# Modulation tiles out of the weight ring: three slots for weights on SP's queue, one slot for modulation tiles on GpSimd's queue

## What is computed

```python
mod = (s_lat @ ada_w[l] + ada_b[l])[:, None, :]      # s_lat = silu(c)
sh1, sc1, g1, sh2, sc2, g2 = jnp.split(mod, 6, axis=-1)
h = modulate(rmsnorm(x, norm1_g[l]), sh1, sc1)       # h * (1 + scale) + shift
...                                                  # h @ w_in: attention, Fourier mix, long convolution
x = x + g1 * (y @ w_out[l])
x = x + g2 * conv_gated_mlp(modulate(rmsnorm(x, norm2_g[l]), sh2, sc2), *ffn)
```

## Time and profile before

| what | value |
|---|---|
| median of 3 runs | 2317.23 us |
| the profiled execution: its own time | 2316.17 us |
| the profiled execution: span of its instructions | 2314.4 us |
| mean granted TensorE clock | 0.986 |
| DMA, all on queue q1 | 467.12 MB, 60.9% of 16 engines' span |

### The profile page before, as it was taken

One profiled execution on the slowest core, in us unless ns is written; L12 is line 12 of the kernel. 1 busy time (PEld: TensorE's weight loads), 2 busy tenths in 40 slices (PEclk: granted clock), 3 DMA queues, 4 the chain that ended last, 5 costly groups with the idle time before them and its releaser, 6 DMA issues.

```text
span 2314.4 us, 37963 instructions
## 1 busy us (share of the span) xinstructions
PE 2202.2 (95%) x16510; PEld 2040.4 (88%) x16510; DVE 1467.1 (63%) x1802; ACT 1029.1 (44%) x1393; POOL 6.2 (0%) x10
## 2 busy tenths in 40 slices
PE   7999999899999997988999799979999999999997
PEld 7889998789899997988788689979999999998885
DVE  6666647757656786767665377776666665555654
ACT  6554334334454553444333354544444443444453
POOL 0000000000000000000000000000000000000000
PEclk9999999999999999999999899989999999999998
DMA  8766565565447876867564655647676766555552
GB/s 295 242 208 193 176 205 182 166 211 164 128 130 253 273 247 200 279 218 252 175 202 154 173 184 184 235 134 264 221 238 219 238 224 205 188 183 198 184 200 91
DMA packets 344260, 469.55 MB, mean 203 GB/s; under 512 B 20445, under 2 KB 318301, under 8 KB 331102
## 3 DMA queue, kind: packets, MB, share of 16 engines
q1 hardware_dynamic: 344094, 467.12, 60.9%
HBM read 465.00 MB, written 2.10 MB: 202 GB/s over the span
## 4 chain that ended last, share of the span: by engine, by line
PE 61%; DVE 6%; ACT 3%; DMA 2%; issue 1%; SPq 1%; DVEq 0%; ACTq 0%
PE ps L1781 14%; PE ps L1779 14%; PE ps L1780 14%; PE ps L1791 3%; PE ps L1793 3%; PE ps L1792 3%; DVE wlo L1087 2%; ACT whi L558 2%; DVE arena L1150 1%; DMA raw<-w_in_dram 1%; SPq L491 1%; PE ps L1802 1%; PE ps L1803 1%; PE ps L1801 1%; PE ps L2142 1%
## 5 line engine op out<-in xcount | busy, mean ns | idle before, releaser
L1087 DVE TENSOR_TENSOR wlo<-raw,whi 128x1024 fp32r<-128x1024 f32 (+1 forms) x668 | 814.3, 1221 | 791.7 <-ACT whi L558 789.7
L558 ACT ACTIVATE whi<-raw 128x1024 fp32r<-128x1024 f32 (+1 forms) x668 | 703.3, 1055 | 1054.5 <-PE ps L1781 836.8
L1779 PE MATMUL ps<-phi,whi 128*128 128x256 f32 (+2 forms) x3744 | 1084.7, 290 | 23.8 <-DVE wlo L1087 15.6
L1780 PE MATMUL ps<-plo,whi 128*128 128x256 f32 (+2 forms) x3744 | 1057.5, 282 | 0.0
L1781 PE MATMUL ps<-phi,wlo 128*128 128x256 f32 (+2 forms) x3744 | 1057.1, 282 | 0.0
L1779 PEld LDWEIGHTS ps<-phi,whi 128*128 128x128 f32 (+1 forms) x3744 | 709.3, 189 | 62.8 <-issue 33.4
L1780 PEld LDWEIGHTS ps<-plo,whi 128*128 128x128 f32 (+1 forms) x3744 | 706.5, 189 | 8.2 <-issue 7.1
L1781 PEld LDWEIGHTS ps<-phi,wlo 128*128 128x128 f32 (+1 forms) x3744 | 709.8, 190 | 0.3
L1150 DVE SCALAR_TENSOR_TENSOR arena<-raw,cst,arena 128x1024 f32<-128x1024 f32 x120 | 153.5, 1280 | 3.4 <-DMA raw<-ada_w_dram 0.3
L1791 PE MATMUL ps<-whi,dhi 128*128 128x512 f32 x352 | 136.9, 389 | 0.0
L1793 PE MATMUL ps<-wlo,dhi 128*128 128x512 f32 x352 | 136.9, 389 | 0.0
(11 more groups left out here) (340 smaller groups left out, 2347.9 us busy)
## 6 DMA issues: line engine op xcount, KB each, us to landing
raw<-w_in_dram SPq DMA_DIRECT2D x151, 1024.0 KB, 6.1
raw<-ada_w_dram SPq DMA_DIRECT2D x96, 1024.0 KB, 5.0
raw<-ffn_w_up_dram SPq DMA_DIRECT2D x88, 1024.0 KB, 5.1
raw<-ffn_w_down_dram SPq DMA_DIRECT2D x44, 1024.0 KB, 5.2
raw<-w_out_dram SPq DMA_DIRECT2D x32, 1024.0 KB, 6.1
raw<-w_branch_dram SPq DMA_DIRECT2D x16, 1024.0 KB, 5.6
arena<-xT_dram SPq DMA_DIRECT2D x4, 544.0 KB, 6.5
arena<-ctxT_dram SPq DMA_DIRECT2D x1, 2048.0 KB, 10.0
```

The lines of the kernel that those rows point to most:

```text
L558: nc.scalar.activation(whi[c % 4][:, 0:w], src, ACT.Copy).then_inc(S("split_hi"), 1)
L1087: v.tensor_tensor(wlo[c % 4][:, 0:w], src, whi[c % 4][:, 0:w].bitcast(F32), ALU.subtract).then_inc(S("split_lo"), 1)
L1779: mm(o, wh[:, k], xk, start=st, stop=False)
L1780: mm(o, wh[:, k], yk, start=False, stop=False)
```

## The change

`RING` is 3, and all its entries are weights; a fourth buffer `tile` of the same size holds one modulation tile at a time, so the memory used is the same. SP no longer issues tiles. GpSimd does, all 96 in order, on its own DMA queue: tile 0 after the first chunk's product, tile n after tile n-1 has been used. Tiles 0 to 3 stand in its list ahead of the wait for `pl_lo` and the three memsets, tiles 4 to 95 behind them. TensorE and VectorE wait for `ada_in` = 16 (n+1) instead of the ring's semaphore.

```diff
-RING = 4
+RING = 3
...
 def ada_tile_at(u, off, sum_at=None):
     n = len(ADA_SLOT)
-    pair = CHUNK[C0[u]:C0[u + 1]][-1][1] == 1
-    ADA_AT[u + pair, 0 if pair else 1] = n
...
-        if (_u, _h) in ADA_AT:
-            ENTRY["ada", ADA_AT[_u, _h]] = len(RELEASE)
-            _n = ADA_AT[_u, _h]
-            RELEASE.append(("ada_mm", _n + 1) if _n < ADA_PE else ("ada_acc", ada_done(_n)))
-            LOADED.append(1 + (LOADED[-RING] if len(LOADED) >= RING else 0))
...
         raw = [sb(f"raw{i}", [128, RW]) for i in range(RING)]
+        tile = sb("tile", [128, RW])
...
-            def load_ada(u, h):
-                if (u, h) in ADA_AT:
-                    n = ADA_AT[u, h]
-                    e = ENTRY["ada", n]
-                    slot_free(e)
-                    sp.dma_start(raw[e % RING][:, :].unsqueeze(1), w_ada[:, n % 16:n % 16 + 1, D * (n // 16):D * (n // 16) + D])\
-                        .then_inc(S(f"loaded{e % RING}"), 16)
...
+            def load_tile(n):
+
+                if n == 0:
+                    pool.wait_ge(S("mm"), 1)
+                elif n <= ADA_PE:
+                    pool.wait_ge(S("ada_mm"), n)
+                else:
+                    pool.wait_ge(S("ada_acc"), ada_done(n - 1))
+                nc.gpsimd.dma_start(tile[:, :].unsqueeze(1), w_ada[:, n % 16:n % 16 + 1, D * (n // 16):D * (n // 16) + D])\
+                    .then_inc(S("ada_in"), 16)
+
+            for n in range(4):
+                load_tile(n)
             pool.wait_ge(S("pl_lo"), 16)
             nc.gpsimd.memset(attn, 0.0).then_inc(S("hg_zero"), 1)
             nc.gpsimd.memset(Qt, 0.0).then_inc(S("hg_zero"), 1)
             nc.gpsimd.memset(Kt, 0.0).then_inc(S("hg_zero"), 1)
+            for n in range(4, 96):
+                load_tile(n)
...
             def ada_half(c, n, half):
-                e = ENTRY["ada", n]
                 if half == 0:
-                    dve.wait_ge(S(f"loaded{e % RING}"), 16 * LOADED[e])
+                    dve.wait_ge(S("ada_in"), 16 * (n + 1))
...
             def ada_tile(n):
-                pe.wait_ge(S(f"loaded{e % RING}"), 16 * LOADED[e])
+                pe.wait_ge(S("ada_in"), 16 * (n + 1))
```

More of the change, by code:

```diff
@@ L56 @@
 SH1, SC1, G1, SH2, SC2, G2 = range(SECTIONS)
-ADA_PE, ADA_AT, ADA_SLOT, ADA_HALF, ADA_SUM = 32, {}, {}, {}, {}
+ADA_PE, ADA_SLOT, ADA_HALF, ADA_SUM = 32, {}, {}, {}
 def ada_tile_at(u, off, sum_at=None):
     n = len(ADA_SLOT)
-    pair = CHUNK[C0[u]:C0[u + 1]][-1][1] == 1
-    ADA_AT[u + pair, 0 if pair else 1] = n
     ADA_SLOT[n] = C0[u] + off
@@ L390, in load @@
                         sp.dma_start(dst, src[:, k0 + 8 * h:k0 + 8 * h + 8, c:c + UC]).then_inc(S(f"loaded{e % RING}"), 16)
-                    load_ada(u, h)
-            def load_ada(u, h):
-                if (u, h) in ADA_AT:
-                    n = ADA_AT[u, h]
-                    e = ENTRY["ada", n]
-                    slot_free(e)
-                    sp.dma_start(raw[e % RING][:, :].unsqueeze(1), w_ada[:, n % 16:n % 16 + 1, D * (n // 16):D * (n // 16) + D])\
-                        .then_inc(S(f"loaded{e % RING}"), 16)
             def load_down(u, kt, c):
@@ L1142, in ada_half @@
                     dve.wait_ge(S("mix_tp"), 2)
-                x = raw[e % RING][:, 1024 * half:1024 * half + 1024]
+                x = tile[:, 1024 * half:1024 * half + 1024]
                 by = cst[:, n % 16, 0:1]
@@ L1812, in ada_tile @@
                     pe.wait_ge(S("mod_set"), FIRST_TILE[n])
-                pe.wait_ge(S(f"loaded{e % RING}"), 16 * LOADED[e])
+                pe.wait_ge(S("ada_in"), 16 * (n + 1))
                 for j in range(4):
-                    l = mm(ps[7][32 * j:32 * j + 32, :], cst[:, n % 16, :], raw[e % RING][:, 512 * j:512 * j + 512],
+                    l = mm(ps[7][32 * j:32 * j + 32, :], cst[:, n % 16, :], tile[:, 512 * j:512 * j + 512],
                            start=n % 16 == 0, stop=n % 16 == 15)
```

## The result

The changed kernel takes 2322.32 us (median of 10 runs, 2321.2 to 2329.01) against 2315.92 us for the kernel before beside it (10 runs, 2314.41 to 2318.69). The ratio is 1.003, 95% interval 1.002 to 1.004. It is slower, by 6.4 us, where 8.8 us of gain were forecast; the time lies 0.3 us above the range (2299 to 2322). The profiled execution of the changed kernel has a span of 2320.5 us and took 2322.25 us.

A forecast was written before the change was run, and what follows sets the result against it. TensorE, busy 2202.2 of 2314.4 us, was taken as the bound. Terms of -18.7 (Part 1), +7.3 (Part 4) and +2.6 (Part 5) summed to -8.8 us: 2307.4 from 2316.2 profiled, 2308.4 as median; range 2299 to 2322.

The forecast's parts named there:

- Part 1a: IQ: SP's list freed from tiles, so TensorE's 12.05 us wait for `k_flip` and the low clock after it go; 14.2 us gained.
- 1b: IQ, chunk 360: its weights' load no longer waits for tile 69, so that stall and its clock loss go; 4.5 us gained.
- last step of Part 1: IQ: VectorE's wait of 2 to 4 us for tile 67 is covered by four split chunks ahead of TensorE; no cost.
- Part 5: F, around 950 us and IH: VectorE waits for closely spaced tiles sharing one buffer; 2.6 us lost.
- Part 4: Start: tile 4 is issued behind GpSimd's memsets, so TensorE stalls 8.8 us and its clock falls; 7.3 us lost.
- Part 3: GpSimd's tile loads: 6.6 us from release of `tile` to landing, with 4.7 and 13.0 us as the ends.
- Part 2: Outside IQ: three slots suffice for weights, 11.9 us being there for a landing of 5 to 8.7; costed at nothing.
- (a): Rival, slower: tile waits in VectorE's list in F, G and IH become the bound, from about 8.5 us a tile; 2328, chance 0.14.
- (c): Rival, no change: bias loads or `k_flip` land 6 us later, so IQ's stall stays in part; 2317 us, chance 0.17.
- (b): Rival, faster: tiles land in 4.7 us (2304), or GpSimd also does not hold tile 4 back (2297); chance 0.18.
- (d): Rival: another queue brings no gain, since bandwidth made chunk 352 late; Part 1 would be 0, 2327 us, chance 0.05.

The follow-up runs named there:

- e4: The kernel before, with the 16 bias-table loads, `k_col` and `k_flip` ahead of the weights of IQ's unit 2 instead of unit 3: 2305.59 us, ratio 0.996.
- e6: The changed kernel's three weight slots and one tile buffer, but tiles issued by SP in the order of the kernel before: 2331.59 us, ratio 1.0071.
- e7: Tiles issued by GpSimd as in the changed kernel, but with the shared ring of four slots of the kernel before: 2331.89 us, ratio 1.0068.
- e8: The changed kernel with the 16 bias-table loads, `k_col` and `k_flip` one unit earlier in IQ: 2315.41 us, ratio 1.0003 to the kernel before.
- e10: The changed kernel with tile 4 ahead of the memsets, half tiles from 32 on and the bias table one unit earlier: 2294.62 us, ratio 0.9911.

## Why the prediction was wrong

- **Part 1a and 1b, the gain at `k_flip` and slot 360: right.** 13.65 us for 14.2, 4.05 for 4.5. That SP's list was held by tiles and not by bytes is shown from three sides: e4 gets the gain at `k_flip` by moving the loads, e6 and e7 lose it by taking half of the change. Two details were off: the 0.3 us to spare for `k_flip` became a wait of 0.36 us (it took 7.0 us to land, not 6.5), and chunk 352's load was still late (ScalarE 7.00 us), hidden behind the tiles.
- **The last step of Part 1 failed, and it decided the sign: a wait of VectorE that was put at nothing.** "A wait of 2 to 4 us for it is covered by the four split chunks ahead of TensorE" was wrong twice. The wait was 6.97 us plus 3.15 for the tile behind it, since the tile is asked for while the 16 small loads are out (4.2 us less without them, e8). And split chunks cover only splits: the bias add stood in the same list, and TensorE needed it. 7.06 us there, and 1.8 at slot 364, where VectorE waited 2.51 us for tile 72; I had nothing for either. That is 8.9 of the 14.8 us between the forecast sum of -8.8 and the +6.0 in the trace; without them the changed kernel would have come out some 3 us faster than the one before. Part 5 has 3.6 more of the 14.8, the start with the clock falls behind it 1.3, and the two gains 1.0.
- **Part 5 was undersized:** 2.6 forecast, 6.2 in the trace, and half tiles bring them back. It was the second failed term: of the right kind, at under half its size. I gave each tight pair of tiles a microsecond; the waits were 2.70 us at tile 41, 3.40, 1.68, 1.73 and 4.03 at tiles 46 to 49, 3.74 at 55 and 2.42 at 57. And I priced the idle time alone: from 883 to 1098 us before, 891 to 1113 in the changed kernel, TensorE's idle time grows by 2.5 us and its busy time by 4.5, with the granted clock at 0.98 before and 0.96 after, so the larger part was work at the lower clock.
- **Part 4 was right in its mechanism and nearly in size:** stall 8.40 for 8.8, and 8.2 us at slot 20 for 7.3. The 8.2 are the stall and the clock as worked out (6.5 and 1.7); the 0.9 us taken off for tile 3 did not last, for by slot 18 both kernels stand at 78.33. The further 1.4 at slot 35 is a fall of the clock that e4 and e10 also show, so it isn't the memsets'.
- **Part 3, the latency:** 6.6 taken. From release to landing it was 5.3 to 6.1 us for 56 of the 95 tiles that were released by a use or by the first chunk, up to 8.5 for 37, 10.5 at tile 49 and 11.3 at tile 67. A middle value hid where the costs lie: in IQ with the one tile that met the small loads and the tile behind it, in F to IH with seven tiles that took 5.8 to 10.5 us. The estimate of about 4.4 us from the Trainium skill ("DMA: Bandwidth & Descriptors", "Anatomy of one DMA — SWDGE (gpsimd) path") lies under every whole tile here.
- **Part 2 was right:** ScalarE's waits for loads by `w_in` fall from 47.2 us to 12.2, of which 7.00 are the late chunk 352 in IQ and not the number of slots; TensorE has no new wait on weights.
- **The rivals.** (a) named the kind of loss that won, VectorE's waits for tiles, but asked for 8.5 us and more at every tile and gave the price to F, G and IH; only two tiles stood clearly above 8.5, and the larger part fell in IQ. (c) had the collision of tile 67 with the small loads, but on the wrong victim: `k_flip` was 0.36 us late, and the tile 6.97. (b) falls: GpSimd held tile 4. (d) falls as put, since the stall went while the bytes stayed; but that another queue by itself brings nothing is what e7 shows (the stall for `k_flip` is 11.7 us there against 12.0). That agrees with the Trainium skill, "DMA: Bandwidth & Descriptors", section "Issuing engines are not separate DMA queues".

## What to carry to other kernels

When a transfer gets a buffer and a list of its own, write down for each of its uses when the buffer is released and what else is landing in the next 10 us; and for the engine that will wait, everything that stands behind the wait in its list, and not only the work that is done ahead. A list in order can be freed more cheaply by moving what is urgent ahead in it: one moved block gave 10.3 us without any buffer (e4). If one buffer is all there is, split it, so that the first half is refilled while the second is read.

## What the runs showed that was not expected

- A load of 1 MB that is asked for at the same moment takes 11.0 us beside the small loads of a table and 6.8 us without them, though more bytes went beside it then (the changed kernel and e8).
- Each half of this change alone costs 0.7% (e6, e7), both together 0.3%, and with loads asked for in time they gain 0.9% (e10).
- A stall of 4.70 us cost 7.06: the rest is work at half the granted clock after it (0.53 from 1338 to 1345 us).
